# The second block of a two-block transformer kernel as one program, its modulation matmuls moved, and the gate projections cut into pieces between the links of the recurrence

## The reference, cut to what matters

```
h   = modulate(rmsnorm(x), sh1, sc1)
p   = h @ w_in                       # q, kv latent, index q/k, 1824 rwkv columns, 2x1024 gate columns
att = top-64-of-256 sparse attention with a low-rank k/v (8 heads)
rw  = RWKV-7 recurrence (8 heads of 64, state 64x64 per head), group norm, gate
y   = (sigmoid(gA) * (att @ w_branch_attn) + sigmoid(gR) * (rw @ w_branch_rwkv)) @ w_out
x   = x + g1 * y
h   = modulate(rmsnorm(x), sh2, sc2)
x   = x + g2 * hierarchical_moe(h)   # 32 experts, 1024 x 512, top 2 of one group
```

## Time and profile before

| | |
|---|---|
| median of 3 runs | 1460.09 us (1457.90 to 1460.11) |
| profiled execution, its time | 1459.41 us |
| profiled execution, span of the core | 1457.7 us |
| mean granted TensorE clock | 0.886 of full |
| TensorE matmul / weight load busy | 79% / 46% of the span |
| VectorE / ScalarE / GpSimd busy | 35% / 18% / 3% |
| HBM read | 402.88 MB, 277 GB/s over the span |

### The profile page before, as it was taken

One profiled execution on the slowest core, in us unless ns is written; L12 is line 12 of the kernel. 1 busy time (PEld: TensorE's weight loads), 2 busy tenths in 40 slices (PEclk: granted clock), 3 DMA queues, 4 the chain that ended last, 5 costly groups with the idle time before them and its releaser, 6 DMA issues. The chain is left out here.

```text
span 1457.7 us, 17019 instructions
## 1 busy us (share of the span) xinstructions
PE 1153.3 (79%) x6655; PEld 673.6 (46%) x6655; DVE 507.6 (35%) x1284; ACT 266.2 (18%) x666; POOL 43.2 (3%) x111
## 2 busy tenths in 40 slices
PE   5999869999999795799899996959657567666656
PEld 2788444443343483567777775634122221221212
DVE  1569442222222466758444444242101011010111
ACT  2223212211121212235222220012010100101000
POOL 0000000000000200000111100000000000000000
PEclk8999879999999798888999996979877887787888
DMA  9777636999999793111111010755999999999995
GB/s 373 278 278 273 250 124 272 403 428 428 427 428 383 243 362 122 58 63 54 59 59 51 9 59 1 293 231 224 422 421 422 422 421 422 422 422 422 422 421 230
DMA packets 75155, 404.68 MB, mean 278 GB/s; under 512 B 14075, under 2 KB 15288, under 8 KB 41308
## 3 DMA queue, kind: packets, MB, share of 16 engines
q1 hardware_dynamic: 75100, 403.95, 68.7%
HBM read 402.88 MB, written 1.05 MB: 277 GB/s over the span
## 5 line engine op out<-in xcount | busy, mean ns | idle before, releaser
L1151 PE MATMUL ps<-ring,hT_sb 128*32 128x512 f32 x768 | 119.2, 778 | 71.5 <-DMA ring<-in_expert_w_gate 41.5
L1513 PE MATMUL ps<-ring,hT_sb 128*64 128x512 f32 x448 | 113.2, 595 | 4.2 <-DMA ring<-in_expert_w_gate 2.4
L1151 PEld LDWEIGHTS ps<-ring,hT_sb 128*32 128x32 f32 x768 | 29.0, 137 | 154.9 <-issue 94.0
L1151 PE MATMUL ps<-side,hT_sb 128*32 128x512 f32 x256 | 41.5, 808 | 36.1 <-DMA side<-in_expert_w_up 18.1
L607 PE MATMUL ps<-hT_sb,ring 128*128 128x256 f32 x256 | 61.9, 392 | 2.7 <-ACT hT_sb L352 2.7
L1163 PE MATMUL ps<-ring,tmp 128*32 128x512 f32 x384 | 49.2, 659 | 18.5 <-DMA ring<-in_expert_w_down 18.5
L1760 PE MATMUL ps<-hT_sb,ring 128*128 128x256 f32 (+1 forms) x240 | 61.5, 417 | 0.1
L1217 ACT ACTIVATE hT_sb<-ps,modc 128x128 f32<-128x128 f32 x72 | 27.1, 457 | 188.8 <-PE ps L1134 188.8
L1513 PEld LDWEIGHTS ps<-ring,hT_sb 128*64 128x64 f32 x448 | 35.3, 137 | 55.9 <-issue 51.8
L1255 DVE TENSOR_TENSOR tmp<-ps,tmp 128x512 f32<-128x512 f32 x8 | 5.5, 692 | 154.4 <-ACT tmp L1225 154.4
L1521 PE MATMUL ps<-ring,tmp 128*64 128x512 f32 x256 | 56.7, 595 | 0.0
(11 more groups left out here) (515 smaller groups left out, 1906.7 us busy)
## 6 DMA issues: line engine op xcount, KB each, us to landing
ring<-in_expert_w_gate SPq DMA_DIRECT2D x12, 4096.0 KB, 34.5
ring<-in_expert_w_up SPq DMA_DIRECT2D x12, 4096.0 KB, 34.8
ring<-in_expert_w_down SPq DMA_DIRECT2D x12, 4096.0 KB, 33.3
ring<-in_expert_w_down SPq DMA_DIRECT2D x16, 2048.0 KB, 15.9
ring<-in_expert_w_up SPq DMA_DIRECT2D x16, 2048.0 KB, 18.3
ring<-in_expert_w_gate SPq DMA_DIRECT2D x12, 2048.0 KB, 19.4
side<-in_ada_w SPq DMA_DIRECT2D x20, 1024.0 KB, 6.4
ring<-in_w_in SPq DMA_DIRECT2D x9, 2048.0 KB, 8.5
```

Source lines behind the costliest of these rows:

```text
L1151: last = pe.matmul(bank[es, :], xg[:, c, es], w[:, e, c % 4, :], start=(c == 0), stop=(c == KC - 1))
L1513: last = pe.matmul(bank[e * SLOTS:(e + 1) * SLOTS, :], xg[:, c, e * SLOTS:(e + 1) * SLOTS], dst(e, j, par)[:, c, :], start=(c == 0), stop= ...
```

## The change

All seven blocks become functions (`project_tensor`, `sparse_tensor`, ..., `merge_tensor`, and so for each engine), called one after another inside one single block; the two `give_back()` between them are gone, and single-event semaphores are merged into counted ones (`COUNTED`, `at(event, n)`). Where a stage relied on the end of a block it now has explicit waits. Apart from that:

```diff
 def sum_ada2_cols(v, k):            # sum_ada2_rows likewise
+    if k == 0: ins = v.tensor_scalar(xn_sb[:, :], w, s, None, ALU.mult)      # no zeros, no bias rows
+    else: ins = v.scalar_tensor_tensor(xn_sb[:, :], w, s, xn_sb[:, :], ALU.mult, ALU.add)
+def gate_row2(pe, i, bank, bias):
+    pe.matmul(bank[:, :], ones[:, :], g_b[:, i // 2, n:n + 512], start=True, stop=False)
+    pe.matmul(bank[:, :], ones[0:1, :], bias[0:1, n:n + 512], start=False, stop=True)
 # project, SP
-    p2_load 0..3; 4 bias rows; krep x4, wi_w, kv_up; load_ada2 2, 3; wait pj_q 2; p2_load 4; load_ada2 4..7; p2_load 5
+    p2_load 0, 1; krep x4, wi_w, kv_up; p2_load 2; load_ada2 2, 3; p2_load 3; load_ada2 4; wait pj_q 2; p2_load 4; load_ada2 5..7; p2_load 5
 # project, GpSimd: the memsets of gate_rows and xn_sb are gone
 # project, TensorE
-SHIFT_BANKS = [m % 4 for m in range(SHIFT_NOW)] + [7, ...]
+SHIFT_BANKS = [0, 1, 2, 3, 4, 7, ...]
 # project, ScalarE (the squares and roots of the norms come from sparse)
     q copies; kv copy
+    Square of q; Square of the latent x2
     wait pj_qi; copy; wait pj_ki; two copies
+    wait lat_ms; Sqrt (lat_root); wait q_ms; Sqrt (q_root)
 # project, VectorE
-    wait bias DMAs; for k in range(8): [shifted_before(k - 6)]; sum_ada2_rows(k); sum_ada2_cols(k)
-    shifted_before 2..4
+    for k in range(2): sum_ada2_rows(k); sum_ada2_cols(k)
+    wait lat_sq; wait lat_root; scale the latent; head_norm(q)       # from sparse
+    for k in range(2, 8): [shifted_before(k - 5) if k >= 5]; sum_ada2_rows(k); sum_ada2_cols(k)
+    shifted_before 3, 4
 # sparse, TensorE, dots(u)
+    if u < 4: pe.wait_ge(sem("mixed_done"), u + 1)
 # prepare, ScalarE, first instruction
+    act.wait_ge(sem("mixed_done"), 15); act.wait_ge(sem("sa_o"), 16)
 # recur, TensorE
-GATE_AFTER = (0, 10, 11)
+GATE_STEPS = ({0: (0, 2), 1: (2, 5), 2: (5, 8)}, {3: (0, 3), 4: (3, 6), 5: (6, 8)}, {9: (0, 3), 10: (3, 8)})
-def gate_bank(i): return ps[(3, 3, 7)[i % 3]][:, P:2 * P]
+def gate_bank(i): return ps[(3, 7, 3)[i % 3]][:, P:2 * P]
 # scan, TensorE
-    between the chunks: gate_row(0..3), mod_columns(0), mod_columns(1)
     for t in range(NT):
         pe.wait_ge(sem("y_normed"), t + 1)
+        if t == 0: gate_row2(pe, 0 and 1, ps[0 and 1], bias_mix)
         4 transposes
+    pe.wait_ge(sem("g2_out"), 1); mod_columns2(pe, 0)
 # merge, TensorE
+    wait or_done; ... after the output projection: wait y3_x 1; mod_columns2(pe, 1)
+    after router_tensor: gate_row2 2 and 3
 # merge, VectorE: + wait modc2_psum 2, two small operations on modc, ahead of the last norm
 # route, GpSimd: the memsets of the tables wait for branch_out 8 only
```

More of the change, by code:

```diff
@@ new lines, in sum_ada2_rows, with load_gate_bias @@
+            ins.then_inc(sem("ada2_rows_summed"), 1)
+        def load_gate_bias(sp, i, dst):
+            m = (2, 5)[i]
+            sp.dma_start(dst, inp["ada_b_2"][0:1, m * D:(m + 1) * D]).then_inc(sem(f"g2_bias{i}"), 16)
+        def gate_row2(pe, i, bank, bias):
+            n = i % 2 * 512
+            pe.wait_ge(sem(f"g2_bias{i // 2}"), 16)
+            pe.matmul(bank[:, :], ones[:, :], g_b[:, i // 2, n:n + 512], start=True, stop=False)
+            pe.matmul(bank[:, :], ones[0:1, :], bias[0:1, n:n + 512], start=False, stop=True).then_inc(sem("g2_psum"), 1)
@@ new lines, in gate_out2, with mod_columns2 @@
+        def gate_out2(act, i, bank):
+            act.wait_ge(sem("g2_psum"), i + 1)
+            act.activation(g_b[:, i // 2, i % 2 * 512:(i % 2 + 1) * 512], bank[:, :], ACT.Copy).then_inc(sem("g2_out"), 1)
+        def mod_columns2(pe, n):
+            vec = xn_sb[:, n * D:(n + 1) * D].rearrange("p (q c) -> p c q", c=KC)
+            for c in range(KC):
+                last = pe.matmul(ps[0][:, c:c + 1], vec[:, c, :], ones[:, 0:1], start=True, stop=True)
+            last.then_inc(sem("modc2_psum"), 1)
@@ L1340, in _, with route_vector @@
                     act.activation(d12, d12, ACT.Exp).then_inc(sem("d12_exp"), 1)
-                @block.vector
-                def _(v):
+                    for i in range(2, 4):
+                        gate_out2(act, i, ps[i])
+                def route_vector(v):
                     v.wait_ge(sem("prio"), k + 5)
@@ L1746, in build @@
         SHIFT_NOW = 5
-        SHIFT_BANKS = [m % 4 for m in range(SHIFT_NOW)] + [7, 4, 7, 5, 6, 4, 7, 7, 7, 7]
+        SHIFT_BANKS = [0, 1, 2, 3, 4, 7, 4, 7, 5, 6, 4, 7, 7, 7, 7]
         LATE_SHIFT = 11
@@ L1804, in build, with project_sync @@
         chunk_of = gate_t[:, P:P + 4]
[L1806 to L1809, removed]
+        if True:
+            def project_sync(sp):
+                for i in range(2):
                     p2_load(sp, i, p2(i), w_cols(w_in, *pieces[i]))
[L1811 to L1814, removed]
                 for r in range(4):
@@ L1989, in build, with sparse_sync @@
         gates_sb = p2(GATE0).rearrange("p (k t) (w n) -> p w k t n", t=NT, w=4)
-        with nc.Block() as block:
-            @block.sync
-            def _(sp):
+        if True:
+            def sparse_sync(sp):
                 sp.wait_ge(sem("pj_shift"), 8)
@@ L2510, in _, with recur_tensor @@
                     pool.wait_ge(sem("i_spread"), u + 1)
[L2512 to L2513 removed]
+            def recur_tensor(pe):
                 def start_(u):
@@ L2609, in _, with recur_scalar @@
                         fb()
-                        if k in GATE_AFTER:
-                            gate_product(3 * pair + GATE_AFTER.index(k))
-            @block.scalar
-            def _(act):
+                        for i, part in enumerate(GATE_STEPS):
+                            if k in part:
+                                gate_product(3 * pair + i, *part[k])
+            def recur_scalar(act):
                 def steps(u):
@@ L2796, in _ @@
                 pe.wait_ge(sem("gated"), 8)
-                pe.wait_ge(sem("modc_ready"), 4)
                 for t in range(NT):
                     pe.wait_ge(sem("y_normed"), t + 1)
+                    if t == 0:
+                        for i in range(2):
+                            gate_row2(pe, i, ps[i], bias_mix)
                     for c in range(4):
@@ L2803, in _, with scan_scalar @@
                 last.then_inc(sem("yT_psum"), 1)
-            @block.scalar
-            def _(act):
+                pe.wait_ge(sem("g2_out"), 1)
+                mod_columns2(pe, 0)
+            def scan_scalar(act):
                 load_sqrt(act, 3)
-                for i in range(4):
-                    act.wait_ge(sem("g2_psum"), i + 1)
-                    act.activation(g_b[:, i // 2, i % 2 * 512:(i % 2 + 1) * 512], ps[7][:, :], ACT.Copy).then_inc(sem("g2_out"), 1)
                 for t in range(NT):
@@ L2815, in _, with scan_vector @@
                     act.activation(st7[:, 8 * t:8 * t + 8], st7[:, 8 * t:8 * t + 8], ACT.Sqrt).then_inc(sem("y_root"), 1)
-            @block.vector
-            def _(v):
+                for i in range(2):
+                    gate_out2(act, i, ps[i])
+            def scan_vector(v):
                 def gate_attn(m):
```

553 lines of the change are left out of this document (301 added, 252 removed).

## The result

The kernel with the change takes 1473.49 us (median of 4 runs, 1471.38 to 1473.65); the kernel before, on the same chip, 1459.78 (1457.90 to 1460.11). The ratio is 1.0096, 95% interval [1.0082, 1.0110]: slower by 13.7 us. The forecast said slower, 1466, by 6.5. The sign held; the size was less than half of what came. The time lies inside the stated range of 1455 to 1475, but near its upper end, and the first expert product came at 1011.31, past the 1009 at which the forecast said that it falls.

A forecast was written before the change was run, and what follows sets the result against it. No one engine was taken to bound the kernel; in each stage the wait ending last did. Terms +13.8 - 2.5 + 11.65 - 13.2 + 2.85 - 6.05 = +6.55 on 1459.41 gave 1465.96 us, range 1455 to 1475.

The forecast's parts named there:

- Step 3: Recurrence: gate projections in pieces between links lengthen seven pairs by 1.55 us each and the last by 0.8: +11.65 us.
- Step 1: Projection and entry of the sparse stage: norms ahead of modulation chunk 2 wait for ScalarE's roots, delaying the weight stream: +13.8 us.
- piece 4: Projection: this 2 MB transfer of input weights, queued between modulation loads 4 and 5, costs some 5.3 us.
- the alternative I set under "bounds", 7.8: Projection: +7.8 us instead of +13.8 if piece 4 does not hold modulation load 5 up.
- Step 5: Moved modulation work (gate rows, column sets) delays the transposes, the rwkv branch and the last norm: +2.85 us.
- Step 4: Scan: without gate rows and column sets the state chain bounds, 20.0 us instead of 33.2: -13.2 us.
- step 2: Sparse stage to preparation: tanh waits only for the last chunk and attention unit, so TensorE goes on earlier: -2.5 us.
- Step 6: Barriers removed, scan to merge -4.2 us and merge to routing -1.85 us: -6.05 us.
- A: Rival, links 1 to 10 of each recurrence pair: pieces fill pauses, -11.4 for +11.65, time 1443; chance 0.10.
- B: Rival: piece 4 does not hold up load 5, and clock stays up in preparation and branch: 1458 to 1461; chance 0.22.
- C: Rival: pieces cost 16 for 11.65, gate rows at half clock 6 for 2.85, one further late load: 1475; chance 0.08.

The follow-up runs named there:

- e5: The change plus unread matmuls, ten behind link 0 and ten behind the maps of each recurrence pair: 1469.24 us, ratio 1.0060.
- e12: The change plus unread matmuls only behind link 0, ten in each recurrence pair: 1472.18 us, ratio 1.0083.
- e1: The change with the recurrence's gate products whole again behind links 0, 10 and 11, instead of in pieces: 1456.06 us, ratio 0.9971.
- e3: The change with ScalarE's two square roots for the latent and q norms put ahead of the index copies: 1463.04 us, ratio 1.0027.
- e7: The change with piece 4 of the input weights loaded behind modulation load 7 instead of between loads 4 and 5: 1470.34 us, ratio 1.0065.
- e8: The change with the matmul work removed from the scan put back as idle work into an unread bank: 1488.10 us, ratio 1.0198.
- e4: The change with whole gate products and ScalarE's square roots ahead of the index copies: 1445.66 us, ratio 0.9909.
- e6: e4 with modulation chunks 2 and 3 summed before the norms of the latent and q on VectorE: 1435.69 us, ratio 0.9840.
- e9: e6 with piece 4 loaded behind modulation load 7, and chunks 5 to 7 summed ahead of shift steps 0 to 2: 1431.97 us, ratio 0.9802.
- e10: e9 with the second of three gate products in pieces of one or two contraction chunks behind links 1 to 7: 1434.64 us, ratio 0.9834.
- e11: The change plus unread matmuls only behind the maps, ten in each recurrence pair: 1477.19 us, ratio 1.0123.

## Why the prediction was wrong in size

The chain was right, and so was the wait named in each of the six steps; the prices were not, and the clock in the preparation and the recurrence was put at no change. The sum missed 8.97 us at the first expert product. Largest first:

- **Step 3, the recurrence: +15.63 for +11.65. This is the step that failed.** The dispatch of the links was right: measured from the start of the first projection, link 2 at 4.8, link 3 at 6.4, solve at 13.8, next pair 21.1 after the last (forecast 4.77, 6.36, 13.89 and 21.3). What failed is that the durations were all taken from a pair at clock 1.00, while the same text said that the first gap and the slot before `i_end` would "stand empty". Three of eight pairs then ran partly at half clock, 3 x 1.64 = 4.9 (e5 and e12 take it away; e1 takes all). The places cost 10.7, a little under forecast. (One reading in the working is off without changing its result: `i_end` comes 19.99 - 17.97 = 2.02 later by its own numbers, not 2.96.)
- **Step 1: +16.64 for +13.8.** Up to the shifted products it is +3.29, where the forecast had 0 ("TensorE's list up to there is unchanged"); from there it is 13.35 for 13.8. Of the 3.29, 1.2 arises in code ahead of the change (block two starts at 484.60; in the profiles of the other kernels, with the same code up to there, at 482.67 to 486.46; before at 483.39), 1.8 is the product of q at a granted clock of 0.88 instead of 1.00, and 0.3 the entry. The first two differ from one profile to the next: the product of q took 13.8 in seven profiles of kernels with the change and 15.3 to 15.6 in five. Loads, piece 4 and the wait for the root are shown by e3 and e7; the alternative I set under "bounds", 7.8, fell.
- **Step 5: gate rows.** They stood at half clock throughout (clock 0.50), 7.96 us for my 6.9, since the 0.86 for two such matmuls at full clock was too little (two take 0.95 in the scan of before, 854.72 to 855.67 at clock 1.00, and 1.99 here), and held the transposes to 922.12; outputs to branch gained 1.34 instead of 2.5. Branch to logits cost 0.63 where 1.15 was forecast.
- **Preparation: +0.95, not forecast.** It came in every kernel with the change (34.30 or 34.31); the `w`/`a` products are longer (6.05 for 4.94), at a granted clock of 0.60 instead of 0.74 over them. So the clock comes back later there although the pause ahead of the stage is gone; why stays open.
- **Step 4: -13.02 for -13.2, step 2: -2.73 for -2.5.** Right, the first shown by e8. **Step 6:** the routing's VectorE came 14.89 later where the logits came 16.76 later: -1.87 for -1.85, of which 1.24 reach the first expert product.
- **Given back later:** 1.4 us within the experts.

The rule of the Trainium skill (page "TensorE: Matmul & The Clock Gate", section "What's actually happening") would have had the branch at the high clock from its start, as it is now preceded by busy matmuls. It did not come in the change; window of the branch's first 6 us, and its row:

```profile
927.52:933.50 5.98, 5.98 (x16) 4.79 (x17) 1.02 (x3) 0.00 (x0) 0.00 (x0) 0.52 0.85 313
```

```profile
927.52 16.90 PE L2939 MATMUL ps<-side,ring 128*128 128x256 f32 x64
```

16.90 us, against 16.89 before. TensorE had been busy without a pause from 914.16 on, at a granted clock of 0.50. That one-column matmuls are busy time and still do not raise the clock is what the earlier trace rows had shown. The moment of the rise is not fixed, though. In e5, with the same instructions from the scan on, it comes earlier, and the branch takes 15.71:

```profile
921.83:927.81 5.98, 5.98 (x21) 5.04 (x22) 1.57 (x5) 0.00 (x0) 0.00 (x0) 0.72 0.85 301
```

In e4, e6, e9 and e10 the branch takes 16.1 to 16.2. So kernels that are alike from the scan on differ by more than 1 us in this product.

Of the rivals: A (pieces fill pauses) fell with pairs of 21.1. B's half on piece 4 fell with e7, and its other half, a clock kept up in preparation and branch, with +0.95 and 16.90. C came nearest in time, for another reason than its own: its 16 for the recurrence stands beside a measured 15.63, but as a price of the pieces, which cost 10.7. That the total stayed inside the range is luck in this sense.

## What to carry to other kernels

Work that lies in a wait does two things: it costs nothing there, and it keeps the wait from being idle. Whoever moves it out should price the emptied slot as well as the new place, from a profile with the granted clock beside each repeat of the loop: here one gap of 1.27 us, refilled with work that nobody reads, was worth 4.9 us. And before a norm, a root or any other two-engine step is moved ahead of a stream, look at what stands before it in the other engine's list: two square roots of 0.2 us each behind the copies of the index columns cost 10.4 us here.

## What the runs showed of the hardware that I had not expected

- In a loop of eight equal pairs, three fall to half clock and five do not, and it is three or none in every profile of this study. In the change and most variants they are pairs three, five and eight, in e7 three, six and eight, in e10 four, six and seven, with no difference in what TensorE does. In the five profiles with the falls of the change (its own, e3, e7, e8, e11), each fall begins less than 1 us behind the wait of 0.96. Which pairs it takes stays open. The busy time of a pair doesn't tell them apart: e10's pairs are busy 17.42 of 19.54 us and fall, those of e12 18.34 of 21.13 and don't.
- The place of an idle slot counts, not only its length: filling 1.43 us behind the maps did nothing, filling 1.27 us, some 2 us later, took away all three falls.
- The stop of 2.8 to 3.0 us inside the output matmuls in e11 and e12 alone, the two kernels with one filler; e5, with both, has none.
